# Latent attention: the score product computed half by half, and the row maximum taken in two halves

## The reference, cut to what matters

```python
def attend(args):
    qn_b, qr_b = args                      # one block of 128 queries, 4 heads
    sc = (jnp.einsum('bqhd,bkhd->bhqk', qn_b, k_nope)
          + jnp.einsum('bqhr,bkr->bhqk', qr_b, k_rot)).astype(jnp.float32) * scale
    p = jax.nn.softmax(sc, axis=-1).astype(v.dtype)
    return jnp.einsum('bhqk,bkhd->bqhd', p, v)
```

## Time and profile before

| | us | share of the span |
|---|---|---|
| median of the runs | 2206.8 | |
| the profiled execution | 2206.76 | |
| its span in the trace | 2205.0 | 100% |
| TensorE matmul busy | 2171.8 | 98% |
| TensorE weight loads busy | 1828.1 | 83% |
| VectorE busy | 1607.8 | 73% |
| ScalarE busy | 975.1 | 44% |
| GpSimd busy | 547.4 | 25% |

### The profile page before, as it was taken

The page is one execution under the profiler, slowest core; times in us unless marked ns, Lnnn a source line. Parts: engine busy times, 40 slices in busy tenths (PEclk is TensorE's granted clock), DMA queues, the critical chain, the costliest instruction groups (busy, mean ns, idle before and its releaser), DMA issues.

```text
span 2205.0 us, 28924 instructions
## 1 busy us (share of the span) xinstructions
PE 2171.8 (98%) x11330; PEld 1828.1 (83%) x11330; DVE 1607.8 (73%) x2050; ACT 975.1 (44%) x1723; POOL 547.4 (25%) x316
## 2 busy tenths in 40 slices
PE   8999999999999999999999999999999999999998
PEld 7888887888888888788888888878888888877887
DVE  5499887975449987796455998788654699878853
ACT  4333335863333333586332333268533333337841
POOL 2122233221122232232111232223211222323310
PEclk9999999999999999999999999999999999999999
DMA  5111121033111112104311111200422111120012
GB/s 183 58 39 44 39 63 48 9 131 131 67 60 46 43 39 63 39 12 162 105 58 67 39 44 39 72 30 20 167 102 77 39 48 44 39 63 29 30 67 96
DMA packets 48422, 140.55 MB, mean 64 GB/s; under 512 B 13184, under 2 KB 13696, under 8 KB 48288
## 3 DMA queue, kind: packets, MB, share of 16 engines
q1 hardware_dynamic: 48288, 138.70, 18.7%
HBM read 120.82 MB, written 17.86 MB: 63 GB/s over the span
## 4 chain that ended last, share of the span: by engine, by line
PE 92%; DVE 4%; ACT 2%; issue 1%; DMA 0%; SPq 0%; POOL 0%; DVEq 0%; ACTq 0%
PE ps L547 48%; PE ps L819 15%; PE ps L768 7%; PE ps L803 5%; PE ps L783 5%; PE ps L652 2%; PE ps L626 2%; PE ps L640 2%; DVE accC L1431 2%; PE ps L701 1%; PE ps L284 1%; PE ps L745 1%; PE ps L557 1%; PE ps L798 1%; ACT PTb L1218 1%; ACT Pb L1210 1%
## 5 line engine op out<-in xcount | busy, mean ns | idle before, releaser
L547 PE MATMUL ps<-hT,stat 128*128 128x512 f32 x4416 | 1052.8, 393 | 0.8 <-DVE Qst L1350 0.8
L547 PEld LDWEIGHTS ps<-hT,stat 128*128 128x128 f32 x4416 | 817.2, 188 | 164.4 <-issue 2.9
L895 POOL TENSOR_TENSOR stat<-raw,stat 128x1024 fp32r<-128x1024 f32 x92 | 250.2, 2719 | 867.2 <-ACT stat L1046 867.2
L1431 DVE SCALAR_TENSOR_TENSOR accC<-uC,parT,accC 128x1024 f32<-128x1024 f32 x240 | 421.3, 1792 | 2.6
L819 PE MATMUL ps<-woR,catR 128*128 128x512 f32 x1488 | 342.5, 390 | 0.0
L819 PEld LDWEIGHTS ps<-woR,catR 128*128 128x128 f32 x1488 | 277.9, 188 | 57.0
L1614 DVE TENSOR_REDUCE bnb<-ps 128x1 f32<-128x1024 f32 x128 | 156.1, 1219 | 43.0 <-PE ps L768 42.3
L1218 ACT ACTIVATE PTb<-ps 128x512 fp32r<-128x512 f32 x256 | 139.1, 596 | 80.9 <-PE ps L783 78.9
L1350 DVE TENSOR_TENSOR PTb<-ps,PTb 128x512 fp32r<-128x512 f32 x256 | 163.2, 678 | 13.0 <-ACT PTb L1218 12.0
L1210 ACT ACTIVATE Pb<-ps,bnb 128x1024 f32<-128x1024 f32 x128 | 143.2, 1118 | 20.9 <-DVE bnb L1614 19.9
L803 PE MATMUL ps<-PTb,Vb 128*128 128x256 f32 x1024 | 151.3, 292 | 0.0
(11 more groups left out here) (196 smaller groups left out, 2782.0 us busy)
## 6 DMA issues: line engine op xcount, KB each, us to landing
raw<-w_in SPq DMA_DIRECT2D x100, 512.0 KB, 3.5
y<-xs SPq DMA_DIRECT2D x31, 512.0 KB, 2.6
raw<-w_out SPq DMA_DIRECT2D x24, 512.0 KB, 3.5
xs<-x SPq DMA_DIRECT2D x16, 512.0 KB, 3.5
xs<-y SPq DMA_DIRECT2D x16, 512.0 KB, 3.5
xd<-x SPq DMA_DIRECT2D x8, 512.0 KB, 8.9
ropeT<-rope SPq DMA_DIRECT2D x4, 1024.0 KB, 5.7
rbc<-latent_factors SPq DMA_DIRECT2D x8, 512.0 KB, 4.9
```

Source lines behind the costliest of these rows:

```text
L547: last = mm(ps[:, 2 * (c % 2) + h, cols], w[:, a, k, :], hT[:, h, b, k, cols], start=(k == 0 and (a, b) == (0, 0)), stop=(k == KD - 1 and ...
L895: pool.tensor_tensor(dst[:, 1], src, dst[:, 0].bitcast(F32), ALU.subtract).then_inc(q["wlo"], 1)
L1431: last_tap[j] = conv.add(stt(accC[:, j, :], uC[:, j, t:t + T], w, accC[:, j, :], ALU.mult, ALU.add))
```

## The change

Two edits that belong together, and a four-column scratch tile `bmx` for them. `b_scores` runs the half in the outer loop, so that the first three matmuls finish bank one of the pair (new semaphore `bs_half`) and the last three bank two (`bs_mm`). `b_max` reduces each half by itself as soon as that half is signalled, into a column of `bmx`, waits for both, and takes the minimum of the two negated maxima into `bnb`. Nothing else is moved. `tt` is VectorE's tensor_tensor.

```diff
-                 "bs_mm": NB, "bm_ok": NB, ...
+                 "bs_mm": NB, "bs_half": NB, "bm_ok": NB, ...
...
-                        for a, b in three:
-                            for half in range(2):
+                        for half in range(2):
+                            for a, b in three:
                                 last = mm(pair(u + 1)[:, half * HALF:(half + 1) * HALF], Q[0:rows, a, i * P:(i + 1) * P],
                                           Kk[0:rows, b, half * HALF:(half + 1) * HALF],
                                           start=((a, b) == (0, 0)), stop=((a, b) == (1, 0)))
-                        last.then_inc(q["bs_mm"], 1)
+                            last.then_inc(q[("bs_half", "bs_mm")[half]], 1)
...
                     def b_max(u):
-                        dve.wait_ge(*got("bs_mm", u + 1))
-                        dve.tensor_reduce(bnb[:, u:u + 1], pair(u + 1), AX.X, ALU.max, negate=True).then_inc(q["bm_ok"], 1)
+                        m = 2 * (u % 2)
+                        if u >= 2:
+                            dve.wait_ge(*got("bm_ok", u - 1))
+                        for half in range(2):
+                            dve.wait_ge(*got(("bs_half", "bs_mm")[half], u + 1))
+                            own.add(dve.tensor_reduce(bmx[:, m + half:m + half + 1], pair(u + 1)[:, half * HALF:(half + 1) * HALF],
+                                                      AX.X, ALU.max, negate=True))
+                        own.wait()
+                        tt(bnb[:, u:u + 1], bmx[:, m:m + 1], bmx[:, m + 1:m + 2], ALU.min).then_inc(q["bm_ok"], 1)
```

More of the change, by code:

```diff
@@ L239, in build @@
         brc = sm("brc", NB)
+        bmx = sm("bmx", 4)
         lss = sm("lss", 2)
@@ L304, in build @@
                  "k_hi": HEADS, "k_lo": HEADS, "q_hi": HEADS, "q_lo": HEADS, "qrope_ok": HEADS, "pw_mm": 2, "pw_ok": 2, "wx_ld": 32,
-                 "bs_mm": NB, "bm_ok": NB, "be_ok": NB, "br_ok": NB // 2, "bt_mm": 2 * NB, "bpt_hi": 2 * NB, "bpt_lo": 2 * NB,
+                 "bs_mm": NB, "bs_half": NB, "bm_ok": NB, "be_ok": NB, "br_ok": NB // 2, "bt_mm": 2 * NB, "bpt_hi": 2 * NB, "bpt_lo": 2 * NB,
                  "bo_mm": NB // 2, "bo_tmp": NB // 2, "bo_ok": NB // 2,
```

## The result

The changed kernel takes 2243.35 us (median of 4 runs, 2243.11 to 2244.86) against 2206.62 us for the kernel before in the same comparison: ratio 1.0167, 95% interval 1.0155 to 1.0180. The change costs 36.7 us. I had forecast 4.4 us slower, with a range that ended at 2216.5.

A forecast was written before the change was run, and what follows sets the result against it. TensorE was taken to bound the kernel, with late maxima stalling it only in some odd units. 2.6 + 1.0 + 0.8 = 4.4 us on 2206.76 us gave 2211.1, say 2211 us, range 2207.5 to 2216.5.

The forecast's parts named there:

- What bounds the kernel: Loop: TensorE's matmuls busy throughout the steady 26.64 us; ScalarE comes last in even units, VectorE in odd ones.
- The order of the matmuls: Six score matmuls per unit, half by half: no cost, 0.2266 us a matmul either way, under 1 us in all.
- The reduction cut in two: VectorE's maximum: two 512-column reductions take 1.28 us (ends 1.21 and 1.40) against 1.21 for one of 1024 columns.
- The wait and the minimum: Behind the two reductions: 0.03 us wait plus 0.15 minimum, so maximum ready after 1.46 us instead of 1.21.
- The term 0.15: Duration in us taken for the minimum of the two columns, from the nearest small instruction's 0.146 us.
- My signs of being wrong: 512-column reduction not near 0.68 us, wait costing far from 0.1, or TensorE's matmuls changing their spacing.
- The Trainium skill's page VectorE: DVE Perf Modes (The DRAIN you can't avoid) against the rows: Semaphore in a chain: free by the page, minimum 0.11 us sooner, sum about 2 us instead of 4; forecast followed rows.
- The sum without the minimum's waiting: Whole kernel: 16 x 0.16 + 4 x 0.25 + 8 x 0.1 = 4.4 us slower, giving 2211.1 us.
- units 15, 17, 21 and 31: Odd units without slack, VectorE late after combinations into partitions 64 to 127: 0.16 us each, 16 times, 2.6 us.
- unit 19: After unit 18, where VectorE waits for ScalarE's copy for head 3: 0.25 us each, four times, 1.0 us.
- unit 11: With unit 23, recovering from a place without slack, some 0.1 us to spare: 0.1 us each, eight times, 0.8 us.
- VectorE becomes the bound of the steady part: Rival, chance 0.18: reductions don't overlap, maximum 0.37 us later, steady odd units stall too, some 9 us, 2216.

The follow-up runs named there:

- split_even: merge_reduce with the cut kept in even units only; odd units have the earlier kernel's one 1024-column reduction: 2205.69 us, ratio 0.9996.
- split_odd: merge_reduce with the cut kept in odd units only; even units have the earlier kernel's one 1024-column reduction: 2211.40 us, ratio 1.0021.
- order_only: The kernel before with only the six score matmuls reordered half by half, one signal and one 1024-column reduction: 2207.03 us, ratio 1.0000.
- merge_reduce: The changed kernel with the two halves' maxima joined by a one-input tensor_reduce in place of the two-input minimum: 2211.09 us, ratio 1.0020.

## Why the prediction was wrong

*What bounds the kernel:* right. TensorE carries the loop, ScalarE comes last in even units and VectorE in odd ones; `split_even` and `split_odd` show it.

*The order of the matmuls:* right, nothing that can be told (order_only).

*The reduction cut in two:* right, 1.27 to 1.29 us for the pair where I took 1.28.

*The wait and the minimum:* this is the step that failed. "The nearest small instruction takes 0.146 us": it has two inputs in SBUF as well, but none of its 64 instances was held up by GpSimd (more on this below). I gave the minimum its size and not its neighbour. The term 0.15 measured 0.16 us in 92 of 128 places and 0.23 to 2.26 in the other 36. The busy time of the 128 minima is 58.4 us instead of 128 x 0.16 = 20.5: 37.9 us of waiting. Of these 4 x 1.73 = 6.9 stand at unit 0, 4 x 0.19 = 0.8 at unit 28 and 30.2 in odd units.

What TensorE feels of it I read from the starts of its first transposes, against the trace of merge_reduce. At unit 0 the transposes stand behind the second gate, and the gate behind the minimum. From GpSimd's first cast in the loop to the transposes it is 369.40 - 363.17 = 6.23 us, before 368.83 - 363.52 = 5.31: 0.9 us a pass, 3.6 in all. Of the 30.2 us some 2.2 are hidden (0.08 us at unit 23, 0.16 each at 25, 27 and 29), and the fall of the clock in three passes adds some 2. Together about 33.6, and the spans of the two profiled executions differ by 2242.7 - 2209.1 = 33.6 us; the account closes to some 0.4 us, since the changed kernel's first loop also began 0.35 us sooner (363.17 against 363.52 before). The medians differ by 2243.35 - 2211.09 = 32.3 us; the profiled execution was the longest of the four, with the lowest clock (0.997 against 0.998 and 0.999).

My signs of being wrong named the reduction, the wait and the spacing of the matmuls; the minimum's own duration was not among them.

*The Trainium skill's page VectorE: DVE Perf Modes (The DRAIN you can't avoid) against the rows* (a semaphore in a chain costs nothing, or 0.11 us): the row was right here, the joining instruction starts 0.03 us behind the reductions (444.92 after 444.89). By this sentence of the Trainium skill the sum would have been 16 x 0.05 + 4 x 0.14 = 1.4 us, less than the 2 that I gave. Beside the 32 us all this was small.

*The sum without the minimum's waiting:* right. merge_reduce, which differs from the change only in how the two columns are joined, took 2211.09 us where my sum for the change was 2211.1. By TensorE's first transposes in its trace against those before, units 15, 17, 21 and 31 lose 0.16 us each, as in the sum (2.5 us of 2.6), unit 19 0.19 where I had 0.25, unit 11 0.17 and unit 23 nothing where I had 0.1 each. So the main term is right by itself, and the agreement to the last tenth is luck in the small ones.

*The rivals:* "VectorE becomes the bound of the steady part" came nearest to the truth in its effect, a maximum more than 0.32 us late in steady odd units, but its mechanism (no overlap of the reductions) and its end of 0.37 us were not what happened. None of my bounds for the minimum looked at GpSimd at all, though its 2.40 us subtractions stand beside the odd maxima of units 21 to 29 in the trace of the kernel before.

That trace showed the price too, on instructions ahead of the loop that I had no reason to cost. L1431 is a scalar_tensor_tensor with two tensor inputs in SBUF:

```profile
L1431 DVE SCALAR_TENSOR_TENSOR accC<-uC,parT,accC x240: 1269/1282/3467, 97.7 to 1926.8; 128x1024 f32<-128x1024 f32 x120
...
272.83 3.38 POOL L895 TENSOR_TENSOR stat<-raw,stat 128x1024 fp32r<-128x1024 f32 x1 [9.87 <-ACT stat L1046]
274.72 2.58 DVE L1431 SCALAR_TENSOR_TENSOR accC<-uC,parT,accC 128x1024 f32<-128x1024 f32 x1
```

64 of the 240 start while GpSimd's L895 runs. They take 2.31 to 3.47 us, and each ends 1.08 to 1.09 us behind GpSimd's end. The other 176 take at most 1.31 us. Another one:

```profile
349.63 4.75 POOL L914 TENSOR_TENSOR cLo<-accC,cHi 128x1024 fp32r<-128x1024 f32 x2 [3.33 <-ACT cHi L1166]
...
353.44 2.02 DVE L1592 TENSOR_TENSOR qrF<-qrF 128x1024 f32<-128x1024 f32 x1
```

A VectorE addition of two SBUF tiles, started while GpSimd ran (until 354.38), took 2.02 us; the other tensor_tensors of 128 x 1024 take 1.2 us. It too ends 1.08 us behind GpSimd.

The same trace also bounds the theory. Not every GpSimd instruction holds VectorE:

```profile
276.17 2.63 POOL L904 TENSOR_TENSOR brs<-bvar,expo 128x8 f32<-128x8 f32 x1
278.78 1.64 POOL L881 TENSOR_TENSOR brs<-bvar,expo 128x8 f32<-128x8 f32 x1
...
279.13 0.15 DVE L1463 TENSOR_TENSOR dsm<-dsm,dex 128x2 f32<-128x2 f32 x1
```

L904 and L881 are powers of eight columns. Four of the 64 instances of the earlier trace rows run inside L881 and take 0.149 to 0.152 us, and four of L1431 start inside L904 with 1.48 us of it left and take 1.28 us. All GpSimd instructions that held VectorE here work on 256 columns or more. Why these small ones let it through no run here shows.

The Trainium skill states the rule, on the page SBUF — State Buffer. VectorE and GpSimd share one pair of SBUF ports, and whichever instruction starts first keeps it for the whole instruction (section SBUF: two separate sides). A VectorE instruction with two SBUF inputs contends with a GpSimd instruction that reads SBUF, and tensor_reduce never does (section Who interferes with whom). The runs of the loop agree: 2.26 us against 0.16 for the minimum, 0.155 us throughout for the joining reduction, and the minimum ending 0.01 to 0.02 us behind GpSimd. The eight-column powers don't: they read SBUF too and kept nothing from VectorE to their end. That the ports are the cause is the Trainium skill's account; the runs show who waits and until when. With this rule and the GpSimd rows of the trace, a price for the minimum's wait could have stood in the sum.

## What to carry to other kernels

Cost a small VectorE instruction by what it must wait for, not by its size: with two tensor inputs in SBUF it can wait out nearly a whole GpSimd instruction, here up to 2.2 us for an operation of 0.16, so look in the timeline for what GpSimd does at that very place, and join two columns with a reduction over both (one input) instead. A cut that lets an engine start early pays only in the units where that engine is early; here that was the half where another engine was the late one. If a two-input instruction can't be avoided, shorter GpSimd instructions bound its wait.

## What the runs showed of the hardware that I had not expected

- The wait does not shrink with VectorE's data: one element per partition waited up to 2.2 us beyond its own 0.16. On GpSimd's side the powers of eight columns held nothing up for 1.6 to 2.6 us, subtractions and casts of 256 columns and more did.
- It starts and ends sharply. Of 32 minima in the first pass nine were longer than 0.16 us, each ending 0.01 to 0.02 us behind a GpSimd instruction.
- GpSimd lets VectorE in between two back-to-back instructions of its own (0.27 us for the minimum at 449.02 with pieces of some 0.7 us), unless the next one has started first: at unit 21 it had, by 0.01 us, and the minimum took 0.74 us.
- TensorE's granted clock fell to 0.50 for 3.4 us behind a stand of 2.08 us in three of the four passes, and not in the second, after the same stand.
- A tensor_scalar with its second operand as a per-partition scalar in SBUF does not wait for GpSimd, but takes 0.214 us where the two-column reduction takes 0.155.
